# Compression, compressed scores and decode attention moved into the loop over 48 head couples of a hybrid decoder layer

## The reference

```
x   = x + 0.5 * rmsnorm(swiglu(rmsnorm(x)))              # FFN 1, width 2816
q, k, v, log f, nq, nkv, gates = rmsnorm(x) @ w_in        # 23 tiles of 128 columns
o_fox = forgetting attention, 8 heads of 64 (scores + cum[q] - cum[k], causal)
o_nsa = g0 * compressed + g1 * selected + g2 * window attention, 8 query heads on 2 kv heads
x   = x + rmsnorm([rmsnorm(o_fox), rmsnorm(o_nsa)] @ w_out)
x   = x + 0.5 * rmsnorm(swiglu(rmsnorm(x)))              # FFN 2
```

## Time and profile before

| | us |
|---|---|
| median of 3 runs | 1250.01 (1247.6 to 1250.06) |
| the profiled execution | 1247.07 |
| its span, first to last instruction | 1245.3 |
| attention loop, first scores to last weighted values | 559.8 to 708.1 |
| tail of attention, to `o_all` | 708.1 to 768.2 |
| first product with `w_out` | about 780 to 788 |

### The profile page before, as it was taken

The page is one execution under the profiler, slowest core; times in us unless marked ns, Lnnn a source line. Parts: engine busy times, 40 slices in busy tenths (PEclk is TensorE's granted clock), DMA queues, the critical chain, the costliest instruction groups (busy, mean ns, idle before and its releaser), DMA issues.

```text
span 1245.3 us, 23642 instructions
## 1 busy us (share of the span) xinstructions
PE 1175.5 (94%) x9650; PEld 1079.6 (87%) x9650; DVE 534.9 (43%) x787; ACT 426.3 (34%) x740; POOL 135.6 (11%) x132
## 2 busy tenths in 40 slices
PE   8999999999999999999999756999999999999994
PEld 6999999999998799995655422888999999999994
DVE  4434332343333653545277645545434323343334
ACT  6222222232244632225265523444222212232332
POOL 0110100011111000322011100120110100011110
PEclk9999999999999999999999976999999999999997
DMA  6222223222123223226150062131322232232221
GB/s 270 102 88 81 86 79 108 102 102 75 69 88 110 85 97 143 69 78 217 51 172 2 3 187 102 35 102 35 102 91 78 77 102 96 99 102 77 76 85 69
DMA packets 46002, 117.95 MB, mean 95 GB/s; under 512 B 4154, under 2 KB 21818, under 8 KB 39874
## 3 DMA queue, kind: packets, MB, share of 16 engines
q1 hardware_dynamic: 42738, 110.95, 26.3%
q10 hardware_dynamic: 3184, 5.88, 1.2%
HBM read 110.93 MB, written 7.97 MB: 95 GB/s over the span
## 4 chain that ended last, share of the span: by engine, by line
PE 88%; DVE 7%; ACT 2%; issue 2%; DMA 1%; DVEq 0%; SPq 0%; ACTq 0%
PE ps L1328 75%; PE ps L1455 2%; PE ps L1472 2%; PE ps L1488 2%; PE ps L1503 1%; PE ps L1337 1%; DVE row_max L1077 1%; DVE UT L917 1%; DVE H L921 1%; DVE XL L897 1%; PE ps L1463 1%; PE ps L1630 1%; PE ps L1421 0%; DMA RAW<-in_w_gu 0%; DMA KW<-in_win_k 0%
## 5 line engine op out<-in xcount | busy, mean ns | idle before, releaser
L1328 PE MATMUL ps<-XH,WH 128*128 128x260 f32 x1904 | 389.1, 285 | 8.3 <-DVE XL L897 8.1
L1328 PE MATMUL ps<-XH,WL 128*128 128x260 f32 x1904 | 383.5, 283 | 0.0
L1328 PE MATMUL ps<-XL,WH 128*128 128x260 f32 x1904 | 382.8, 283 | 0.0
L409 ACT CAST WH<-RAW 128x1024 fp32r<-128x1024 f32 (+2 forms) x183 | 174.8, 956 | 530.7 <-PE ps L1328 526.1
L1328 PEld LDWEIGHTS ps<-XH,WH 128*128 128x128 f32 x1904 | 294.6, 188 | 15.0 <-DVE XL L897 12.1
L1328 PEld LDWEIGHTS ps<-XH,WL 128*128 128x128 f32 x1904 | 293.4, 188 | 0.0
L1328 PEld LDWEIGHTS ps<-XL,WH 128*128 128x128 f32 x1904 | 292.7, 188 | 0.0
L412 DVE TENSOR_TENSOR WL<-RAW,WH 128x1024 fp32r<-128x1024 f32 (+2 forms) x183 | 203.7, 1113 | 157.9 <-ACT WH L409 156.6
L1328 PE MATMUL ps<-UL,WH 128*128 128x260 f32 x704 | 141.9, 283 | 0.0
L1328 PE MATMUL ps<-UH,WL 128*128 128x260 f32 x704 | 141.5, 282 | 0.0
L1328 PE MATMUL ps<-UH,WH 128*128 128x260 f32 x704 | 141.3, 282 | 0.0
(11 more groups left out here) (233 smaller groups left out, 934.5 us busy)
## 6 DMA issues: line engine op xcount, KB each, us to landing
RAW<-in_w_gu SPq DMA_DIRECT2D x44, 1024.0 KB, 4.8
RAW<-in_w_down SPq DMA_DIRECT2D x16, 768.0 KB, 4.8
RAW<-in_w_in SPq DMA_DIRECT2D x11, 1024.0 KB, 4.8
RAW<-in_w_down SPq DMA_DIRECT2D x16, 640.0 KB, 4.3
KF<-in_fox_k SPq DMA_DIRECT2D x16, 256.0 KB, 4.4
VF<-in_fox_v SPq DMA_DIRECT2D x16, 256.0 KB, 5.4
RAW<-in_w_out SPq DMA_DIRECT2D x4, 1024.0 KB, 4.9
H<-in_x SPq DMA_DIRECT2D x4, 520.0 KB, 7.2
```

What stands on the lines that cost most here:

```text
L409: nc.scalar.copy(WH[:, par, 0:width], RAW[:, slot, j, 0:width]).then_inc(w_hi, 1)
L1328: q = nc.tensor.matmul(ps[:, 2 * slot + half, 0:HALF], w[:, par, cols], x[:, kt0 + kt, half * HALF:(half + 1) * HALF], start=first and kt ...
```

## The change

Nothing is computed otherwise in substance; the tail of attention is taken apart, and its pieces (guests) run inside the loop, in banks 4 and 5, between `scores` of a couple and `turn_p` of an earlier one. In a guest's step PE waits until both banks are copied out, does the guest's matmuls, and waits until DVE or ACT has taken the result out of the banks. The softmax arithmetic between two guests is appended to later steps of DVE, ACT and POOL (`follow`). For that,
- the hidden layer is laid out anew: `X` holds the windows twice, the second time shifted by one position, so that a matmul contracts two positions (128 rows) and 64 do for 128; `w1` comes as two compact 64-column blocks for each kind (rows of 256 B). SP issues 38 transfers per kind where there were 19;
- compressed scores are made with the queries as the stationary side (32 matmuls of 128 x 32 values), so that their transposes go; the compressed values are added by a matmul at the end of each tile's `weigh` instead of by DVE;
- ACT and DVE copy the turned units before the exponentials and the scaling (not in a guest's step, where it is as before);
- memory is laid out so that decode operands can be loaded during the loop, `PT_SLOTS` is 6, and `w_out` is streamed from step 36 on.

```diff
-KF_SLOTS = 5
-BURST_AT = 14
+AT_HIDDEN, AT_CMP_KV, AT_CMP_SCORES, AT_CMP_BACK = 13, 15, 17, 25
+AT_PICK, AT_FOX_KEYS, AT_NSA_KEYS, AT_TURN, AT_VALUES, AT_DECODED = 18, 22, 26, 30, 33, 36
...
-PT_SLOTS = 8
+PT_SLOTS = 6
... SP
+            for n in (0, 1):
+                for kv in range(HKV):
+                    part = slice(64 * kv, 64 * kv + 64)
+                    sp.dma_start(W1[n][part, :, :], I["w1"][n, part].rearrange("p (j two) c -> p two j c", two=2)[
+                        :, kv, :, part]).then_inc(sem(f"cmp_in{n}"), 16)
+                for half in range(2):
+                    part = slice(64 * half, 64 * half + 64)
+                    for g in range(NPAGE):
+                        c = SEQ + g * PAGE - half
+                        sp.dma_start(X[n][part, :, c:c + PAGE], ...).then_inc(sem(f"cmp_in{n}"), 16)
...
+            for n in (2, 3, 4):
+                fox_keys(n)
             sp.wait_ge(sem("cmp_hid"), 1)
+            for n in (0, 1, 5, 6, 7):
+                fox_keys(n)
...
-            sp.wait_ge(sem("att_pv"), PAIRS)
+            sp.wait_ge(sem("att_pv"), 16)
...
-            sp.wait_ge(sem("d_scored"), 2)
+            sp.wait_ge(sem("d_ot"), 2)
             stream(mid + n_in, KT // 2)
... ACT
             def attention():
                 for m in range(PAIRS + 3):
+                    if m >= 3 and m not in GUESTS:
+                        turn_out(act, nc.scalar.copy, 2 * (m - 3) + 1, "att_odd_out")
                     if m < PAIRS:
+                        exponentials(m)
+                    if m in GUESTS:
+                        guest(m)
                         turn_out(act, nc.scalar.copy, 2 * (m - 3) + 1, "att_odd_out")
+                    follow(m)
... DVE
                     if m < PAIRS:
+                        largest(m)
+                    if m >= 3 and m not in GUESTS:
+                        turn_out(dve, nc.vector.tensor_copy, 2 * (m - 3), "att_even_out")
                     if 1 <= m <= PAIRS:
+                        divide(m - 1)
+                    if m in GUESTS:
+                        guest(m)
                         turn_out(dve, nc.vector.tensor_copy, 2 * (m - 3), "att_even_out")
+                    follow(m)
... DVE follow
+                if m == AT_CMP_SCORES:
+                    nc.vector.reduce_max(cmax, SCM, AX.X)
+                elif m == AT_PICK + 1:
+                    ... 8 copies into QBF, 8 into QBN, 8 into KF
+                elif m == AT_CMP_SCORES + 3:
+                    ... reduce_sum(csum), reciprocal, product with the gates
+                elif m == AT_NSA_KEYS:
+                    ... three reduce_max ; AT_NSA_KEYS + 2 and + 3: scaling, PN, PCX
+                elif m == AT_VALUES:
+                    ... two reduce_sum into OS
... PE
+                if br == 1 and i == QT - 1:
+                    nc.tensor.matmul(ps[:, 6 + t % 2, :], VCZ[:, t - 4, :], PCT[:, (t - 4) // 2, :], start=False, ...)
+            def hidden_windows():
+                for n in (0, 1):
+                    pe.wait_ge(sem(f"cmp_in{n}"), 16 * (2 + 2 * NPAGE + 2 + 2))
+                    for j in range(CMP_LEN // 2):
+                        for kv in range(HKV):
+                            q = nc.tensor.matmul(ps[64 * kv:64 * kv + 64, 4 + n, 0:N_WIN], W1[n][:, j, :],
+                                                 view(X[n][:, kv, :], 2 * j, [[CMP_STRIDE, N_WIN]]), ...)
+                q.then_inc(sem("cmp_hid"), 1)
+                pe.wait_ge(sem("hid_k_out"), 1)
+                pe.wait_ge(sem("hid_v_out"), 1)
+            def compressed_scores():
+                for i in range(QT):
+                    for h in range(HN):
+                        q = nc.tensor.matmul(ps[:, 4 + h % 2, c:c + 32], QXN[part, h // 2, i * P:i * P + P],
+                                             KC[part, h // 4, :], start=True, stop=True)
+                q.then_inc(sem("cmp_scored"), 1)
+                pe.wait_ge(sem("cmp_rows_out"), 1)
...
                     if m < PAIRS:
                         scores(2 * m)
-                    if m == BURST_AT:
-                        windows()
+                    if m in GUESTS:
+                        guest(m)
                     if 3 <= m < PAIRS + 3:
                         turn_p(2 * (m - 3))
```

More of the change, by code:

```diff
@@ L559, in fox_keys @@
[L559 to L571, removed]
@@ L777, in ropes_free, with exponentials @@
                 act.wait_ge(sem("stack_lo"), 2)
+            def exponentials(m):
+                act.wait_ge(sem("att_max"), m + 1)
+                for v in (2 * m, 2 * m + 1):
+                    W = P * (unit(v)[3] + 1)
+                    if v >= PR_SLOTS:
+                        act.wait_ge(sem("att_turned"), v - PR_SLOTS + 1)
+                    nc.scalar.activation(weights(v)[:, 0:W], ps[:, score_bank(v), 0:W], ACT.Exp,
+                                         bias=row_max[:, v:v + 1], accum_out=row_sum[:, v:v + 1]).then_inc(
+                        sem("att_exp"), 1)
@@ L1295, in _ @@
+            def attention():
+                for m in range(PAIRS):
+                    for u in (2 * m, 2 * m + 1):
+                        if unit(u)[3] < DVE_SCALES:
+                            scale_p(pool, nc.gpsimd.tensor_scalar, u)
+                    follow(m)
             ffn(0, "a")
             project()
-            pool.wait_ge(used, IT_OUT)
-            nc.gpsimd.memset(QBF[:, :, :], 0.0)
-            nc.gpsimd.memset(QBN[:, :], 0.0).then_inc(sem("qb_cleared"), 1)
+            nc.gpsimd.memset(QBN[:, :], 0.0)
@@ new lines, in pick, with fox_keys @@
+            def pick():
+                pe.wait_ge(sem("lf_new"), 1)
+                for c in range(4):
+                    q = nc.tensor.matmul(ps[0:ROWS, 4, c * DEC:(c + 1) * DEC],
+                                         const("pick")[0:64, c * ROWS:(c + 1) * ROWS], fg_new[0:64, :],
+                                         start=True, stop=True)
+                q.then_inc(sem("d_picked"), 1)
+                pe.wait_ge(sem("gb_out"), 1)
+            def fox_keys():
+                pe.wait_ge(sem("qb_filled"), 1)
+                pe.wait_ge(sem("kf_new"), 1)
+                pe.wait_ge(sem("kf_in"), 16 * NPAGE)
+                for m in range(DEC // 2):
+                    for t in range(4):
+                        for n in (2 * m, 2 * m + 1):
+                            b = KF_ORDER[n]
+                            q = nc.tensor.matmul(ps[ROWS * (t % 2):ROWS * (t % 2) + ROWS, 4, 0:NEWK][rows_of(b)],
+                                                 only(QBF[:, t, :], b), KF[n][:, t, :], start=m == 0 and t < 2,
+                                                 stop=m == 3 and t >= 2, skip_group_check=True)
+                q.then_inc(sem("kf_scored"), 1)
+                pe.wait_ge(sem("sf_out"), 1)
@@ new lines, in decoded, with guest @@
+            def decoded():
+                pe.wait_ge(sem("d_o"), 1)
+                for g in (0, 1):
+                    nc.tensor.transpose(ps[0:DH, 4, g * ROWS:(g + 1) * ROWS], OS[:, g, :],
+                                        ident[0:ROWS, 0:ROWS]).then_inc(sem("d_ot"), 1)
+                pe.wait_ge(sem("o_all"), 1)
+            def guest(m):
+                banks_free(m)
+                if m == AT_HIDDEN:
+                    hidden_windows()
+                elif m == AT_CMP_KV:
+                    compressed_kv()
+                elif m == AT_CMP_SCORES:
+                    compressed_scores()
+                elif m == AT_CMP_BACK:
+                    compressed_back()
+                elif m == AT_PICK:
+                    pick()
+                elif m == AT_FOX_KEYS:
+                    fox_keys()
+                elif m == AT_NSA_KEYS:
+                    nsa_keys_of_decode()
+                elif m == AT_TURN:
+                    turn_decode()
+                elif m == AT_VALUES:
+                    decode_values()
+                elif m == AT_DECODED:
+                    decoded()
```

802 lines of the change are left out of this document (397 added, 405 removed).

## The result

The changed kernel takes 1256.09 us (median of 15 runs, 1252.46 to 1261.01) beside 1247.6 for the kernel before on the same chips (15 runs, 1243.28 to 1251.2): 1.0071 times, interval 1.0052 to 1.0089. It is slower by 0.7%; the prediction had it 1.4% faster. The profiled execution took 1260.31 us with a span of 1258.5, 13.2 more than the span before.

A forecast was written before the change was run, and what follows sets the result against it. PE work was taken to bound the kernel where PE is full (busy 94%), elsewhere the last wait; -58.2 + 33.0 + 7 + 5 + 4 - 7 = -16.2 us gave 1230.9, beside the median 1233.8, stated as 1233; 8-in-10 range 1215 to 1247.

The forecast's parts named there:

- Step 13's matmuls: Hidden layer as guest of the loop's step 13: 32 pairs of matmuls, column halves running together, 9.0 us.
- without pairing: Hidden layer in step 13 if column halves do not run together: 17.8 us instead of 9.6 with start and copy.
- Operands: PE's wait in step 13 for the hidden layer's loads, issued by SP: 2 to 8 us, taken as +5.
- operands late: Rival: DMA at half pace makes the hidden layer wait 12 to 15 us, 1241 to 1244 us; chance 0.09 (1241 to 1247.5).
- Clock: Falls of PE's clock in the loop around step 13 and guests 15 to 18: +4 us, 0 to 10.
- slower rival: Guests keep TensorE at its low clock: no gain left from 20 us at 0.50, 1260 us at 30; chance 0.11.
- New order: Copies before scalings in the loop remove PE's 9.4 us wait but for 2.4: -7 us, between 0 and 8.9.
- the drain: End of the loop, where 2.4 us of PE's 9.4 us wait for DVE's copies was to remain.
- The tail's end: Norm of the outputs starts 3.9 to 4.3 us after the loop, so 1.9 of the removed 60.1 us come back.
- DVE's arithmetic in steps 20 and 21: Softmax arithmetic between guests makes PE wait 5 us there for a turned copy, part of a +7 us term.
- The guests: Tail pieces run inside the loop, steps 13 to 36: +51.9 us, of which 18.9 was there already, so +33.0.
- the prediction's other figure: Step 17's compressed-score matmuls by the Trainium skill's 107 ns load for 128 columns: 6.8 us instead of 4.4.

The follow-up runs named there:

- e1: Changed kernel with the hidden layer's 19 transfers a kind and 128 matmuls of 64x64 as before, but on only two of four tiles: 1254.64 us, ratio 1.0048.
- e2: Changed kernel, hidden layer's moving operand read at a step of 1 value instead of 16 (other windows computed): 1257.3 us in one run.
- e5: Changed kernel with the hidden layer fully as before the change, on all four tiles, two copies each on ACT and DVE: 1238.65 us, ratio 0.9924.
- e7: Changed kernel reading pages 0 to 15 without the page table, by 8 large transfers instead of 64: 1238.25 us, ratio 0.9926.
- e3: Changed kernel plus short bf16 matmuls, results unused, in PE's waits in step 13 and eight of nine other guests: 1245.76 us, ratio 0.9987.
- e6: e5 plus short bf16 matmuls, results unused, in the guests' waits after the hidden layer: 1225.43 us, ratio 0.9841.
- e4: Kernel before the change with only the new order: ACT and DVE copy turned units before exponentials and scaling: 1235.3 us, ratio 0.9893.
- e10: Changed kernel with the old order of copies in couples without a guest: 1260.33 us, ratio 1.0106.
- after: The changed kernel itself, beside the kernel before: 1256.09 us, ratio 1.0071.
- e9: e6 with hidden-layer operands first copied side by side, both copies on DVE, and three KF slot loads moved behind the hidden layer: 1219.66 us, ratio 0.9767.
- e12: Changed kernel, hidden layer's moving operand read at a step of 4 values instead of 16 (other windows computed): 1251.23 us in one run.
- e11: Changed kernel, hidden layer's moving operand read at a step of 2 values instead of 16 (other windows computed): 1255.7 us in one run.

## Why the prediction was wrong, step by step

The sum said -16.2 against the profiled execution; it was +13.2 on the span. Four terms make up most of the 29. About 5 of it are no term at all: by the medians on the same chips the change cost 8.5 us, and the execution that was profiled lies 4.2 above the median. Its steps 0 to 3 took 8.2 us instead of 6.1, with the clock at 0.50 from 560.7 to 567.5, before the first guest.

**Step 13's matmuls: 9.0 foretold, 18.55 measured, +9.5.** The step that failed is "0.14 each, when one alone needs 0.27, so two at a time". I had read 0.14 as two tiles at full rate. It was four tiles at half rate (e1, e2, e5), and two tiles at half rate give what I had called "without pairing", 17.8. The rows of weighted values from which I took the pairing are right, but their moving operand has no step.

**Operands: a wait of 5 foretold, 18.0 measured, +13.** The count of transfers was right. The step that failed is "0.51 to 0.61 each" for a transfer of the same bytes: a half page into 64 partitions took 0.71 to 0.88, and the twelve others 0.6 to 0.7 instead of 0.5, so XV was issued by 616.6, not by 596 to 602. This term and the one before are tied: the slower first kind covers 4.8 us more of the wait, so without the late issue the wait would have been about nothing. As a whole, matmuls and wait of step 13 were to take 14 us and took 36.5. My rival "operands late" had the place and nearly the wait (12 to 15) but the wrong cause, half pace of the DMA engines: their share was 0.36 in this stretch, and e7 moves the same rows in time.

**Clock: 4 foretold (0 to 10), some 10 to 13 measured (e3, e6), +6 to +9.** I saw the mechanism and mis-sized it: "two or three falls at 1.5 to 2 us each". The first two falls alone lasted 20.5 us each, though 14.9 us of the first passed in the wait for XV and cost nothing:

```profile
605.10:625.60 20.50, 5.59 (x40) 4.41 (x42) 0.00 (x0) 0.00 (x0) 0.00 (x0) 0.50 0.33 84
625.60:639.20 13.60, 10.79 (x81) 6.31 (x78) 5.64 (x15) 7.74 (x19) 1.82 (x2) 1.00 0.93 259
639.20:659.70 20.50, 18.13 (x124) 13.73 (x124) 6.70 (x17) 3.70 (x14) 0.87 (x2) 0.50 0.32 86
```

Four more, of 3.4 to 6.9 us, began at 670, 690, 714 and 742, up to step 36. My slower rival was about this. No term decided the sign alone: e5 and e7 keep the low clock and are 0.75% faster than before, and e3, which mends only the clock, is level with it (0.9987 [0.9968, 1.0006]).

**New order: -7 foretold, -13 alone (e4), -4 in this kernel (e10).** The step that failed is "the turn goes to its PE bound, 9.95 to 9.2": busy time of PE, whose ends are modelled, is no bound to 0.2 us, and the turn became 8.99 in e4. Of the 2.4 that I left in the drain 1.3 were gained. In the changed kernel 3.7 of the gain went into the wait for XV; where the rest went is open, the clock being argued and not shown.

Roughly: 9.5 + 13 + 6 to 9, less 6 for the order at the size of e4, is 22 to 26, beside 25 by the medians. With the order at the size of e10, where it gives 3 less than foretold, it is 31 to 35. The terms overlap, since the first kind covers part of the wait and a clock level changes the others, and no run adds them up.

**What held.** The tail's end: from the loop's end to the product with `w_out` it is 15.3 us, 13.3 before, the 1.9 that I had given back. DVE's arithmetic in steps 20 and 21: 4.2 us (5). The guests, read in e6 at full clock (but for 0.8 us at the start of step 22) as step length less that of a couple of the same i: 15 took 4.4 (4.7), 17 took 5.3 (6.2), 18 took 1.4 (1.6), 22 took 5.2 (4.9), 25 took 3.5 (2.7), 26 took 4.6 (4.7), 30 took 4.2 (3.7), 33 took 8.1 (7.8), 36 took 2.4 (2.6); `fox_keys` 3.7 (3.6). Compressed scores took 3.76 us in e6, 0.06 a record over the two row halves, and 7.04 in after at a clock of 0.50. The 3.76 lies below both the 4.4 taken and the 6.8 of the prediction's other figure, and inside its 2.2 to 6.9. It is 0.12 us a record of each half, so whether the load of 128 columns sets their pace while the two halves overlap is open. With windows side by side, operands in time and the clock up, the kernel is at 1219.66: the prediction's 1233 less its own 5 and 4 for wait and clock, and less the 6 by which the order gives more, is 1218. This sum was made after the fact, and part of its closeness is luck: it leaves out the copies and the 5 us that e9 loses at a low clock, and it takes the order at the size of e4, not of e10.

## What to carry to other kernels

A rate read from a trace belongs to its operands as well as to its shape: before a matmul is regrouped, ask how many tiles gave the old rate and whether two reads in a row of the moving operand share 16 bytes; a copy that puts them side by side may cost less than it saves. Count transfers by a duration of the same access pattern, not of the same bytes; here 8 transfers instead of 64 were worth 18 us. Before work is spread into a full loop, count PE's waits in it: here they brought the clock down, and short matmuls in them gave back 10 to 13 us. Try the cheap part (here the order of copies, 1.1%) by itself first: it gave no less than the whole change did with step 13 mended (e4 beside e5).

## What was not expected of the hardware

- fp32 matmuls with 161 moving columns took 4.60, 4.86, 9.37 and 9.31 us per 64 records at steps of 4, 8, 16 and 64 bytes. At the long steps the clock hardly matters: the second kind took 9.10 (e10), 9.24 (after) and 9.41 us (e12) with the granted clock at 0.50 for its first 4.1, 5.6 and 3.2 us, and 9.40 at 1.00 throughout (e3). Without the long step it went from 4.60 to 7.52 (e2, 0.50 for 6.0 us) and from 4.86 to 7.35 (e11, 0.50 for 5.5 us).
- Issuing a transfer of 64 KB took SP 0.598 us in the median when it went to 64 partitions with two rows each, 0.33 to 0.34 for 128 partitions with one. Why is open; e7 shows only that fewer transfers cure it.
- ACT took 4.57 us for a fp32 copy with a 64-byte step of 2592 elements in each partition, DVE 2.36.
